# Full 128 by 128 shapes for the spread of 1/rms, direct squares for the third tile, and a larger weight ring for the second mixer

## The reference, cut to what matters

```
h = h + 0.5 * swiglu(rmsnorm(h, g1), w_gate1, w_up1, w_down1)      # D_FF = 2816
u = rmsnorm(h, g_mix);  proj = u @ w_in                            # 1184 columns
o_mla = latent attention, 8 heads, causal (low-rank q and kv, each with its own rmsnorm, rotary key)
o_swa = sliding-window attention, 8 heads, window 128, sinks, T5 bias
h = h + concat(rmsnorm(o_mla), rmsnorm(o_swa)) @ w_o
h = h + 0.5 * swiglu(rmsnorm(h, g2), w_gate2, w_up2, w_down2)
out = rmsnorm(h, g_final)
rmsnorm(x, g) = x / sqrt(mean(x*x) + eps) * g
```

## Time and profile before

| | value |
|---|---|
| median of 3 runs | 4866.15 us |
| the profiled execution's own time | 4864.43 us |
| its span on the slowest core (core 4) | 4862.9 us |
| spans of the 8 cores | 4849.4 to 4862.9 us |
| mean granted TensorE clock, by core | 0.994 to 0.996 |
| PE busy | 4788.4 us, 98% |
| DVE, ACT, POOL busy | 56%, 39%, 9% |
| PE busy in 1000 to 4300 us, granted clock there | 3300.0 of 3300 us, 1.00 |
| PE busy in 0 to 640 us, and from 4300 us to the end | 591.0 of 640 us, 538.2 of 562.9 us |
| HBM | 162 GB/s over the span |

### The profile page before, as it was taken

One profiled execution on the slowest core, in us unless ns is written; L12 is line 12 of the kernel. 1 busy time (PEld: TensorE's weight loads), 2 busy tenths in 40 slices (PEclk: granted clock), 3 DMA queues, 4 the chain that ended last, 5 costly groups with the idle time before them and its releaser, 6 DMA issues.

```text
span 4862.9 us, 92165 instructions; the slowest of 8 cores (4849.4 to 4862.9 us)
## 1 busy us (share of the span) xinstructions
PE 4788.4 (98%) x28672; PEld 2300.4 (47%) x28672; DVE 2715.9 (56%) x6281; ACT 1906.8 (39%) x3579; POOL 458.4 (9%) x472
## 2 busy tenths in 40 slices
PE   8899999999999999999999999999999999999998
PEld 3344444445444444545444444444544444445444
DVE  4476555545475564654556565555455645655554
ACT  1133545255242433535423253443632324335641
POOL 1200010100101010010010101001010111000000
PEclk9999999999999999999999999999999999999999
DMA  9976664444454454543545454454444545443334
GB/s 196 204 212 149 177 187 151 149 127 159 148 177 147 134 177 139 158 146 119 166 149 175 149 160 152 132 165 150 141 144 144 178 147 174 141 140 118 124 110 142
DMA packets 261591, 748.29 MB, mean 154 GB/s; under 512 B 28576, under 2 KB 45472, under 8 KB 260768
## 3 DMA queue, kind: packets, MB, share of 16 engines
q1 hardware_dynamic: 231968, 645.63, 42.2%
q0 software_dynamic: 28864, 96.74, 8.9%
q10 hardware_dynamic: 288, 0.03, 0.0%
HBM read 713.52 MB, written 73.60 MB: 162 GB/s over the span
## 4 chain that ended last, share of the span: by engine, by line
PE 95%; DMA 3%; DVE 1%; issue 1%; SPq 0%; POOL 0%; ACT 0%; DVEq 0%; POOLq 0%; ACTq 0%
PE ps L610 48%; PE ps L642 24%; PE ps L957 5%; PE ps L1110 5%; PE ps L774 4%; PE ps L977 3%; PE ps L615 1%; PE ps L1010 1%; PE ps L896 1%; DMA sb_slotB<-wd 1%; DMA wd1s<-sb_slotB 1%; PE ps L834 1%; PE ps L1036 1%; PE ps L456 1%; PE ps L1084 1%
## 5 line engine op out<-in xcount | busy, mean ns | idle before, releaser
L610 PE MATMUL ps<-sb_u,sb_slotA 128*128 128x512 bf16 x10688 | 2600.6, 379 | 3.7 <-DMA sb_slotA<-wgu 2.4
L610 PEld LDWEIGHTS ps<-sb_u,sb_slotA 128*128 128x128 bf16 x10688 | 992.4, 98 | 1059.4 <-issue 12.3
L642 PE MATMUL ps<-sb_act,sb_slotB 128*128 128x512 bf16 x5632 | 1318.7, 380 | 7.1 <-DMA sb_slotB<-wd 4.0
L629 DVE SCALAR_TENSOR_TENSOR sb_tb<-sb_tb,ps 128x512 f32<-128x512 f32 x704 | 482.9, 686 | 652.7 <-PE ps L610 281.0
L962 ACT ACTIVATE sb_PT<-ps 128x512 bf16<-128x512 f32 (+3 forms) x1280 | 655.6, 533 | 487.0 <-PE ps L957 399.0
L625 ACT ACTIVATE sb_tb<-ps 128x512 f32<-128x512 f32 x704 | 419.1, 596 | 1069.7 <-PE ps L610 848.5
L642 PEld LDWEIGHTS ps<-sb_act,sb_slotB 128*128 128x128 bf16 x5632 | 537.1, 98 | 614.2 <-issue 15.9
L649 DVE SCALAR_TENSOR_TENSOR sb_h<-ps,sb_h 128x512 f32<-128x512 f32 x544 | 374.7, 690 | 438.8 <-PE ps L642 390.0
L632 DVE TENSOR_TENSOR sb_act<-sb_tb,ps 128x512 bf16<-128x512 f32 x704 | 482.8, 686 | 226.8 <-PE ps L610 181.0
L957 PE MATMUL ps<-sb_QT,sb_KT 128*128 128x512 bf16 (+3 forms) x1280 | 424.6, 347 | 0.0
L482 ACT ACTIVATE sb_sqF<-sb_h 128x512 bf16<-128x512 f32 x384 | 237.7, 627 | 433.7 <-DVE sb_h L1114 182.2
(11 more groups left out here) (132 smaller groups left out, 2901.5 us busy)
## 6 DMA issues: line engine op xcount, KB each, us to landing
sb_slotA<-wgu2s SPq DMA_DIRECT2D x340, 512.0 KB, 3.6
sb_slotA<-wgu1s SPq DMA_DIRECT2D x308, 512.0 KB, 3.9
sb_slotM<-wms SPq DMA_DIRECT2D x273, 256.0 KB, 2.8
sb_slotB<-wd2s SPq DMA_DIRECT2D x120, 384.0 KB, 3.2
sb_slotB<-wd1s SPq DMA_DIRECT2D x112, 384.0 KB, 3.1
sb_slotB<-wd2s SPq DMA_DIRECT2D x124, 320.0 KB, 2.9
sb_slotB<-wd1s SPq DMA_DIRECT2D x112, 320.0 KB, 3.1
outT<-sb_h POOLq DMA_DIRECT2D x30, 1024.0 KB, 7.5
```

What stands on the lines that cost most here:

```text
L610: inst = nc.tensor.matmul(PS[bank][:], lhsT=w[:, a, kc, :], rhs=ub[:, kc, :], start=(kc == 0), stop=(kc == 7))
L629: G.op("dve", [("tb", t), P(gb)], [("tb", t)], lambda: nc.vector.scalar_tensor_tensor(out=tb[:, t, :], in0=tb[:, t, :], scalar=1.0, in1=PS ...
L642: inst = nc.tensor.matmul(PS[bank][:], lhsT=w[:, c, :], rhs=act1[:, a0 + c, :], start=(c == 0), stop=(c == nch - 1))
```

## The change

Four things are edited.

1. `nwFb` and `nwMb` grow from 8 to 128 columns, zeroed once. The transposes of line 445 then have a 128 by 128 operand and give 128 rows, the copy of line 448 moves 128 rows, and `spread` contracts over 128 rows, of which `sel` holds zeros in all but the first 8. Three memsets on DVE are new.
2. `pre_u` of FFN 1 for tile 2 uses the direct form.
3. Mixer 1 has its own ring `ring_m1`: the three slots and eight places in KT's third and fourth quarter.
4. The due times of mixer 1's DMAs are 40 us ahead, not 12.

```diff
-        nwF = sb("nwF", [128, 6, 8], F32)
-        nwFb = sb("nwFb", [128, 2, 8], BF16)
-        nwM = sb("nwM", [128, 6, 8], F32)
-        nwMb = sb("nwMb", [128, 2, 8], BF16)
+        nwF = sb("nwF", [128, 4, 4], F32)
+        nwFb = sb("nwFb", [128, 1, 128], BF16)
+        nwM = sb("nwM", [128, 4, 8], F32)
+        nwMb = sb("nwMb", [128, 2, 128], BF16)
...
-                    inst = nc.tensor.transpose(tp[0:8, g * 128:(g + 1) * 128], nwb[:, g, :], ident[:])
+                    inst = nc.tensor.transpose(tp[:, g * 128:(g + 1) * 128], nwb[:, g, :], ident[:])
...
-                out=trow[0:8, 0:ng * 128], in_=tp[0:8, 0:ng * 128]), 0.2)
+                out=trow[:, 0:ng * 128], in_=tp[:, 0:ng * 128]), 0.2)
...
-                    inst = nc.tensor.matmul(PS[bank][:, j * 128:(j + 1) * 128], lhsT=sel[0:8, j, :],
-                                            rhs=trow[0:8, g * 128:(g + 1) * 128], start=(j == 0), stop=True,
+                    inst = nc.tensor.matmul(PS[bank][:, j * 128:(j + 1) * 128], lhsT=sel[:, j, :],
+                                            rhs=trow[:, g * 128:(g + 1) * 128], start=(j == 0), stop=True,
...
+        G.op("dve", [], [("sel",)], lambda: nc.vector.memset(sel[:], 0.0), 0.3, vt=-4000)
+        G.op("dve", [], [("nwFb",)], lambda: nc.vector.memset(nwFb[:], 0.0), 0.1, vt=-4000)
+        G.op("dve", [], [("nwMb",)], lambda: nc.vector.memset(nwMb[:], 0.0), 0.2, vt=60)
...
+        ring_m1 = ring_m + [(KT[:, 2 + i // 4, 2 * (i % 4):2 * (i % 4) + 2, :].rearrange("p a t -> p (a t)"),
+                             ktk(2 + i // 4, 2 * (i % 4)) + ktk(2 + i // 4, 2 * (i % 4) + 1)) for i in range(8)]
...
-            ring = ring_mk if m_cast[0] else ring_m
+            ring = ring_mk if m_cast[0] else ring_m1 if m_tile[0] == 1 else ring_m
...
-            pre_u(n, 16 * f, u1, ukey1, fpos[0] - 24, f == 1 and (n < 2 or n >= NT - 2))
+            pre_u(n, 16 * f, u1, ukey1, fpos[0] - 24, n >= NT - 2 and f == 1 or n < 2 + (f == 0))
...
-                o.vt = w0 + (w1 - w0) * p / tot - (12.0 if o.kind == "dma" else 0.0)
+                o.vt = w0 + (w1 - w0) * p / tot - ((40.0 if n == 1 else 12.0) if o.kind == "dma" else 0.0)
```

More of the change, by code:

```diff
@@ L462, in build_program @@
         assert addr[0] <= nc.sbuf_usable_end, (addr[0], nc.sbuf_usable_end)
-        G.op("dve", [("ident",)], [("sel",)], lambda: nc.vector.tensor_tensor(
-            out=sel[0:8], in0=ident[0:8, 0:4].unsqueeze(2).to_broadcast([8, 4, 128]),
-            in1=ident[0:8, 4:8].unsqueeze(2).to_broadcast([8, 4, 128]), op=ALU.add), 0.7, vt=-3000)
+        G.op("dve", [], [("sel",)], lambda: nc.vector.memset(sel[:], 0.0), 0.3, vt=-4000)
+        G.op("dve", [], [("nwFb",)], lambda: nc.vector.memset(nwFb[:], 0.0), 0.1, vt=-4000)
+        G.op("dve", [], [("nwMb",)], lambda: nc.vector.memset(nwMb[:], 0.0), 0.2, vt=60)
+        G.op("dve", [("ident",), ("sel",)], [("sel",)], lambda: nc.vector.tensor_tensor(
+            out=sel[0:32], in0=ident[0:32, 0:4].unsqueeze(2).to_broadcast([32, 4, 128]),
+            in1=ident[0:32, 4:8].unsqueeze(2).to_broadcast([32, 4, 128]), op=ALU.add), 0.7, vt=-3000)
         def stat_mm(sq, s, skey, bank, col, first, last, oc=0):
@@ L701, in build_program @@
                              ktk(1 + i // 4, 2 * (i % 4)) + ktk(1 + i // 4, 2 * (i % 4) + 1)) for i in (0, 1, 2, 3, 6, 7)]
+        ring_m1 = ring_m + [(KT[:, 2 + i // 4, 2 * (i % 4):2 * (i % 4) + 2, :].rearrange("p a t -> p (a t)"),
+                             ktk(2 + i // 4, 2 * (i % 4)) + ktk(2 + i // 4, 2 * (i % 4) + 1)) for i in range(8)]
+        m_tile = [0]
         def m_item(i):
-            ring = ring_mk if m_cast[0] else ring_m
+            ring = ring_mk if m_cast[0] else ring_m1 if m_tile[0] == 1 else ring_m
             s = m_cnt[0] % len(ring)
@@ L748, in mixer @@
             G.m = n
+            m_tile[0] = n
             G.slack = SLACK_M if 2 < n < NT - 2 else SLACK_E
```

## The result

The changed kernel takes 4833.0 us as a plain median of seven runs. So taken it is 4828.3 against 4866.15, 38 us less. The ratio, 0.9898 with a 95% interval from 0.9868 to 0.9928, says more than the medians do (0.9922); before has only three runs in it, one of them at 4886. A second comparison with more runs gave 4835.7 against 4870.3, 34.5 less, ratio 0.9946 (0.9923 to 0.9969). By the medians the gain is 34 to 38 us where 41 were forecast. That there is a gain is clear; its size is less sure, as the two intervals together reach from 15 to 64 us.

The account below looks back on a forecast made before the run. PE was taken as the bound, busy 4788.4 of 4862.9 us. Terms -32 (shapes), -6 (squares), -4.6 (mixer 1's loads) and +0.6 (new matmuls) gave -42, forecast 4825 us, range 4806 to 4843.

Parts of the forecast that it names:

- Part 1, the shapes: Spread groups and transposes on PE each lose 0.19 us in full shape; 33.4 us less 1.4, taken as 32.
- The weight loads: Loads of 128 instead of 8 columns for 96 transposes: 9.6 us lost by the skill's formula; the prediction charged nothing.
- Part 2, the third tile's squares: Direct squares remove PE's 7.76 us wait near 165 us and low clock; bounds 0 and 16, taken as 6.
- The sign that the prediction had set for this: New waits of PE for slotB's DMA before 230 us, if the steady gain is right and the early one is not.
- rival B: DMA takes back all that the squares and mixer 1's weight loads give: 4835 us, chance 0.20.
- The Newton wait: PE held 3.91 us at 212.75 by the same chain's Newton part, some 2 more lost to the clock after it.
- The 0.6 for the new one-column matmuls: Cost of 24 more one-column matmuls in the direct squares: between 0 and 1.4 us, taken as 0.6.
- Parts 3 and 4: Mixer 1's loads go into idle DMA time at 440 to 450 us; bounds 0 and 8, taken as 4.6.
- the DVE chain's 2.44: PE's 2.44 us wait for line 869, a DVE chain, was to stay, perhaps with the low clock.
- D: Mixer 1's early loads block SyncE's queue, FFN loads come late and PE starves: slower than before, chance 0.03.
- A: The extra 0.19 us does not go with the shape at all: 4856 us, chance 0.04.
- E: Only one of the two shape costs (spread or transpose) goes: 4839 us, chance 0.06.

Follow-up runs that it names:

- e1: Only the full shapes for transposes and spread (edit 1), on the kernel before: 4836.3 against 4866.3 us, ratio 0.9934.
- e5: Only the transposes in full shape (nwFb and nwMb 128 columns wide), spread still over 8 rows, on the kernel before: 4856.8 against 4869.8 us, ratio 0.9975.
- e11b: Only the spread in full shape (128 rows), transposes still with 8 columns, on the kernel before: 4854.3 against 4870.2 us, ratio 0.9970.

## Why the prediction was right or wrong

- **Part 1, the shapes, was right.** 0.19 a group was right to the hundredth, and the gain of the steady stretch (28.4) is the count times it. The forecast said 32, measured are 30.0. What was off is the deduction for groups that stand where PE waits anyway: I took off 1.4 for ten groups (ten times 0.19 would have been 1.9), but of the 33.4 some 5 belong to the first 700 us, and 1.5 of those came through.
- **The weight loads cost nothing.** The Trainium skill's rule on them (TensorE: Matmul & The Clock Gate, section "LDWEIGHTS (loading the stationary operand)") would have had an estimate of 9.6 us lost, and does not show here: the 96 loads with 128 columns in place of 8 take 98 ns each instead of 82, and PE's starts don't show it; a full transpose is followed after 0.06. Of the two rules of the Trainium skill that the prediction set against each other, the one of TensorEngine Tiling, section "Key Properties" (a change of tiling mode drains the array), is the one that the runs bear out, with 64 rows as with 8 and for columns as for rows. They show the price (0.19) and that the full shape removes it. That the array runs empty in it is the reading that fits; no trace shows the array itself.
- **Part 2, the third tile's squares, is the step that failed.** The mechanism was right: the tanh behind the square, the 7.76 us and the low clock went, and PE was 7 us ahead at 195 us. I then took 6 of 16 as lasting, "a full queue gives only part of that back". It gave back all but 2 by 246 us, and nothing is left at the end (4866.6 against 4866.3). The sign that the prediction had set for this is there: a wait for slotB before 230 us, 5.31 at 211.68. The cast issued 7.7 us earlier in the median of the cores landed no earlier, and with four precasts fewer in the phase it landed 15 to 20 earlier. So here the time of a landing is set mostly by the traffic of the phase and hardly by when it is asked for. I had the row for it (the DMA share of 1.08 and 18.4 us to land) and named it as rival B, and should have followed it. The Newton wait, in the 16 as 3.9 with 2 behind it, stands in the changed kernel and with direct squares alone; only with the precasts moved was it covered. The 0.6 for the new one-column matmuls, for which I said that no row has a price, can be read: four of them take 0.10 from start to start (2140.64 to 2140.74 in the changed kernel), so 24 take 0.6.
- **Parts 3 and 4 were right in size,** 4.6 forecast, 4.7 by the times and 4 to 7 by the traces at 702, with intervals that don't leave out 0; the reason was half wrong, so the hit is in part luck. I put it to the lead into the idle DMA time at 440 us; the lead alone does nothing, and with the ring seven of the loads still go out into the full stretch, at 458 to 469 us (core 0), and take 14 to 18 us to land. They don't hurt since PE needs them later. And I said that the DVE chain's 2.44 stays; it went, since with more places the planner could put twenty of the mixer's matmuls ahead of it. The 2.5 us lost to the low clock there was read from durations: against the durations of four and eight full matmuls, 1.03 and 1.89 in the same timeline, it is 2.2.
- **The rivals.** B came true for part 2 and not for part 3. Its time, 4835, and the forecast's 4825 lie on both sides of the measured gains, which are 4828 and 4832 when both are taken off 4866. D, the slow one, did not show: between 430 and 520 us no core of the changed kernel waits more than 0.3 us for a DMA. A and E are refuted by e1, e5 and e11b.

The time lay inside the range. The size of the change was forecast 41, and is 34 to 38; 6 of the excess are part 2, 2 are part 1.

## What to carry to other kernels

In a stream of full matmuls, a lone one with fewer rows or columns costs about 0.2 us more than its columns say, on its neighbours' starts and not in its own duration; look for it from start to start, and pad with zeros. Where the DMA engines are full, removing a stall moves the stall: count the bytes of the phase before the gain is booked. If a wait comes from a ring of buffers that is too short, more places help without any earlier due time, and an earlier due time without places does not: here the ring alone gave 5.9 us, the lead alone nothing, each known to some 7 us.

## What the runs showed of the hardware that was not expected

- The price of a change of shape did not depend on how much is missing: 0.42 us for a group of four spreads with 8 rows, 0.43 with 64, 0.22 with 128. One transpose with 8 columns pays the same, 0.19.
- With a DMA share above 1, a cast issued 7.7 us earlier (median of the cores) landed at the same time.
- A burst of three precasts (1.0 MB read and 0.5 MB written each) made PE wait 10.1 us for a load in a stretch whose mean DMA share was 0.42: three loads of 384 KB took 16.9 us to land instead of 3.0, although they are issued on another queue (SyncE's) than the precasts (GpSimd's).
